# Two PSUM moves in a three-layer transformer kernel: the banks of the dilated attention, and the second GLA pair's cumulated logarithms

## What is computed

```python
h = x
h = h + hgrn2_mixer(rmsnorm(h), ...)              # 8 heads, chunked linear recurrence
h = h + swiglu_ffn(rmsnorm(h), ...)
h = h + dilated_attention_mixer(rmsnorm(h), ...)  # 3 groups (window, dilation) x 4 heads of 128
h = h + swiglu_ffn(rmsnorm(h), ...)
x = rmsnorm(h)
h = rmsnorm_2(x)                                  # second block: NSA attention beside GLA
merged = gate_a * (nsa_attention(...) @ w_up_nsa) + gate_b * (gla_chunked(...) @ w_up_gla)
x = x + merged @ w_out
x = rmsnorm_2(x + ffn(rmsnorm_2(x)))
```

## Time and profile before

| | |
|---|---|
| median of 3 runs | 2213.12 us (2212.46 to 2219.25) |
| the profiled execution's own time | 2218.95 us |
| its span in the profile | 2217.1 us |
| TensorE busy | 2157.2 us, 97% |
| VectorE, ScalarE, GpSimd busy | 1050.2, 852.3, 1173.3 us |
| granted TensorE clock, mean | 0.99 of 2.4 GHz |
| DMA | 193.3 MB, mean 87 GB/s |

### The profile page before, as it was taken

The page is one execution under the profiler, slowest core; times in us unless marked ns, Lnnn a source line. Parts: engine busy times, 40 slices in busy tenths (PEclk is TensorE's granted clock), DMA queues, the critical chain, the costliest instruction groups (busy, mean ns, idle before and its releaser), DMA issues. The chain is left out here.

```text
span 2217.1 us, 28302 instructions
## 1 busy us (share of the span) xinstructions
PE 2157.2 (97%) x10458; PEld 1779.5 (80%) x10458; DVE 1050.2 (47%) x1483; ACT 852.3 (38%) x1209; POOL 1173.3 (53%) x635
## 2 busy tenths in 40 slices
PE   8999999999999999999999999989999999999997
PEld 6788878888888988778888888778767888888886
DVE  7766774422433047754431446464684344422433
ACT  6565644322233234434321233344664334222222
POOL 5868755554554355535554555473214555554552
PEclk9999999999999999999999999999999999999999
DMA  4112213332332222123332332323101223332331
GB/s 166 58 57 66 65 59 95 95 111 88 95 111 80 86 86 76 58 73 103 95 113 84 97 109 81 126 60 96 67 20 62 100 90 91 102 102 89 95 111 69
DMA packets 52822, 193.30 MB, mean 87 GB/s; under 512 B 6768, under 2 KB 7680, under 8 KB 52480
## 3 DMA queue, kind: packets, MB, share of 16 engines
q1 hardware_dynamic: 50688, 184.95, 26.8%
q10 hardware_dynamic: 2048, 7.19, 0.8%
HBM read 187.92 MB, written 4.19 MB: 87 GB/s over the span
## 5 line engine op out<-in xcount | busy, mean ns | idle before, releaser
L1583 POOL TENSOR_TENSOR w_split<-ring,w_split 128x1024 fp32r<-128x1024 f32 (+3 forms) x327 | 842.8, 2578 | 825.9 <-ACT w_split L1102 825.8
L1102 ACT CAST w_split<-ring 128x1024 fp32r<-128x1024 f32 (+3 forms) x327 | 356.3, 1090 | 1009.0 <-PE ps L414 870.7
L412 PE MATMUL ps<-u_split,w_split 128*128 128x512 f32 x1768 | 707.4, 400 | 15.6 <-DVE u_split L1795 10.7
L414 PE MATMUL ps<-u_split,w_split 128*128 128x512 f32 x1768 | 692.5, 392 | 0.0
L413 PE MATMUL ps<-u_split,w_split 128*128 128x512 f32 x1768 | 692.2, 392 | 0.0
L412 PEld LDWEIGHTS ps<-u_split,w_split 128*128 128x128 f32 x1768 | 334.6, 189 | 93.2 <-issue 18.7
L414 PEld LDWEIGHTS ps<-u_split,w_split 128*128 128x128 f32 x1768 | 334.2, 189 | 71.3
L413 PEld LDWEIGHTS ps<-u_split,w_split 128*128 128x128 f32 x1768 | 334.9, 189 | 69.8 <-issue 3.1
L412 PE MATMUL ps<-hid,w_split 128*128 128x512 f32 x648 | 254.0, 392 | 4.3 <-DVE arena L2080 2.8
L414 PE MATMUL ps<-hid,w_split 128*128 128x512 f32 x648 | 252.7, 390 | 0.0
L413 PE MATMUL ps<-hid,w_split 128*128 128x512 f32 x648 | 252.7, 390 | 0.0
(11 more groups left out here) (312 smaller groups left out, 2608.4 us busy)
## 6 DMA issues: line engine op xcount, KB each, us to landing
ring<-in_w_hgrn SPq DMA_DIRECT2D x32, 512.0 KB, 3.5
ring<-in_w_attn_qk SPq DMA_DIRECT2D x24, 512.0 KB, 3.6
ring<-in_w_merge SPq DMA_DIRECT2D x24, 512.0 KB, 3.2
ring<-in_w_gu0a SPq DMA_DIRECT2D x22, 512.0 KB, 3.5
ring<-in_w_gu0b SPq DMA_DIRECT2D x22, 512.0 KB, 3.5
ring<-in_w_gu1a SPq DMA_DIRECT2D x22, 512.0 KB, 3.6
ring<-in_w_gu1b SPq DMA_DIRECT2D x22, 512.0 KB, 3.5
ring<-in_w_gu2a SPq DMA_DIRECT2D x22, 512.0 KB, 3.6
```

Of the source, the lines that this page charges most:

```text
L412: nc.tensor.matmul(ps[:, bank], ws[:, 0, r, w], act[:, 0, c], start=c == 0, stop=False)
L414: m = nc.tensor.matmul(ps[:, bank], ws[:, 1, r, w], act[:, 0, c], start=False, stop=c == n - 1)
L1102: nc.scalar.copy(ws[:, 0, slot, 0:w], ring[:, r, 0:w]).then_inc(s["w_hi"], 1)
L1583: nc.gpsimd.tensor_tensor(ws[:, 1, slot, 0:w], ring[:, r, 0:w], ws[:, 0, slot, 0:w].bitcast(F32), ALU.subtract).then_inc(s["w_lo"], 1)
```

## The change

In the attention, the query/key tiles 0 to 3 use banks 4 to 7 (`qk_bank`), tiles from 4 on bank `N % 4` as before. Tile 0 waits for the first two value groups, tile 4 for the third, tiles from 8 on for the rotation of the tile four before. The value products go to banks 4, 6 and 7 for groups 0, 1 and 2 (`AO_BANK`), each group after its own copied probabilities. In the output projection the wait for the heads' low parts stands in `attn_out` before the three chunks of each head.

In the GLA part, ScalarE copies the second pair's running sums `la[:, 1]` to bank 3 after the gates' eviction. The second pair's level and end exponents read the row from there; the reference columns are still read from SBUF.

```diff
+        AO_BANK = (4, 6, 7)
+
+        def qk_bank(N):
+
+            return 4 + N if N < 4 else N % 4
...
             def qk_tile(N):
-                if N >= 4:
+                if N >= 8:
                     pe.wait_ge(s["rope_sin"], 2 * (N - 3))
-                elif N == 0:
-                    pe.wait_ge(s["av_ready"], GROUPS * TT)
-                used(unit("attn_qk", N, us, N % 4))
+                elif N % 4 == 0:
+                    pe.wait_ge(s["av_ready"], (3 if N else 2) * TT)
+                used(unit("attn_qk", N, us, qk_bank(N)))
...
                 for c in range(6):
                     g, j, w = c % 3, 2 * second + c // 3, slice(c * P, (c + 1) * P)
+                    if c % 3 == 0:
+                        pe.wait_ge(s["ao_lo"], GROUPS * (j + 1))
...
-                    pe.wait_ge(s["pt_ready"], 3 * j + (n + 1 if g == 0 else 3))
+                    pe.wait_ge(s["pt_ready"], 3 * j + n + 1)
                     for b in range(TT):
-                        o = ps[:, 4 + g, b * P:(b + 1) * P]
+                        o = ps[:, AO_BANK[g], b * P:(b + 1) * P]
...
-                    pe.wait_ge(s["ao_lo"], GROUPS * 2)
                     for k in range(4):
                         attn_out(k)
                 attn_core(j)
-            pe.wait_ge(s["ao_lo"], GROUPS * HPG)
...
+
+            act.wait_ge(s["ngate_ready"], TT)
+            act.wait_ge(s["cum"], HEADS_H + 2)
+            nc.scalar.copy(ps[:, 3], la[:, 1]).then_inc(s["cum"], 1)
...
-            def level_exponents(b, dv, l):
+            def level_exponents(b, dv, l, whole=None):
 
                 m = 1 << l
-                bb = b.rearrange("p (b h m) -> p b h m", h=2, m=m)
+                bb = (b if whole is None else whole).rearrange("p (b h m) -> p b h m", h=2, m=m)
                 x = dv[:, l].rearrange("p (b h m) -> p b h m", h=2, m=m)
-                ref = bb[:, :, 0, m - 1:m].broadcast_to((P, T // (2 * m), m))
+                ref = b.rearrange("p (b h m) -> p b h m", h=2, m=m)[:, :, 0, m - 1:m].broadcast_to((P, T // (2 * m), m))
...
                 for l in {1: (6, 5), 2: (4, 3), 3: (2, 1), 4: (0,)}.get(n, ()):
-                    level_exponents(la[:, 1], gdec, l)
+                    if l == LEVELS - 1:
+                        dve.wait_ge(s["cum"], HEADS_H + 3)
+                    level_exponents(la[:, 1], gdec, l, ps[:, 3])
...
             gather_pair(0, next_pair)
             dve.wait_ge(s["kt_ps"], HEADS_H + 1)
-            end_exponents(la[:, 1], gdec)
+            end_exponents(la[:, 1], gdec, ps[:, 3])
```

More of the change, by code:

```diff
@@ L1340, in take_raw @@
                     act.wait_ge(s["qk_ready"], N - 1)
-                nc.scalar.copy(raw[:, N % 2], ps[:, N % 4]).then_inc(s["raw_ready"], 1)
+                nc.scalar.copy(raw[:, N % 2], ps[:, qk_bank(N)]).then_inc(s["raw_ready"], 1)
             def exps(j, g):
@@ L1378, in _ @@
                     act.wait_ge(s["ao_ps"], 3 * j + n + 1)
-                    nc.scalar.copy(in_order(ao_split[:, 0, g * HPG + j]), by_query(g, ps[:, 4 + g])).then_inc(s["ao_hi"], 1)
+                    nc.scalar.copy(in_order(ao_split[:, 0, g * HPG + j]), by_query(g, ps[:, AO_BANK[g]])).then_inc(s["ao_hi"], 1)
             act.wait_ge(s["qk_ready"], 24)
@@ L1913, in cumulate, with end_exponents @@
                 dve.wait_ge(s["cum"], cnt(it, 1, 1))
-            def level_exponents(b, dv, l):
+            def level_exponents(b, dv, l, whole=None):
                 m = 1 << l
-                bb = b.rearrange("p (b h m) -> p b h m", h=2, m=m)
+                bb = (b if whole is None else whole).rearrange("p (b h m) -> p b h m", h=2, m=m)
                 x = dv[:, l].rearrange("p (b h m) -> p b h m", h=2, m=m)
-                ref = bb[:, :, 0, m - 1:m].broadcast_to((P, T // (2 * m), m))
+                ref = b.rearrange("p (b h m) -> p b h m", h=2, m=m)[:, :, 0, m - 1:m].broadcast_to((P, T // (2 * m), m))
                 nc.vector.tensor_tensor(x[:, :, 0], ref, bb[:, :, 0], ALU.subtract)
                 nc.vector.tensor_tensor(x[:, :, 1], bb[:, :, 1], ref, ALU.subtract).then_inc(s["dec_in"], 1)
-            def end_exponents(b, dv):
+            def end_exponents(b, dv, whole=None):
                 b2 = b.rearrange("p (c t) -> p c t", c=NCH)
+                w2 = b2 if whole is None else whole.rearrange("p (c t) -> p c t", c=NCH)
                 nc.vector.tensor_tensor(dv[:, L_END].rearrange("p (c t) -> p c t", c=NCH),
-                                        b2[:, :, C - 1:C].broadcast_to((P, NCH, C)), b2, ALU.subtract
+                                        b2[:, :, C - 1:C].broadcast_to((P, NCH, C)), w2, ALU.subtract
                                         ).then_inc(s["dec_in"], 1)
@@ L2093, in rope @@
                     src, dst = slice(lower, lower + 64), slice(64 - lower, 128 - lower)
-                    nc.vector.tensor_tensor(tsin[dst, N % 2], ps[src, N % 4], sin_a[src], ALU.mult
+                    nc.vector.tensor_tensor(tsin[dst, N % 2], ps[src, qk_bank(N)], sin_a[src], ALU.mult
                                             ).then_inc(s["rope_sin"], 1)
@@ L2153, in ao_rest @@
                     low = ao_low(g, j).rearrange("p b (m r) -> p b m r", r=RESIDUES)
-                    nc.vector.tensor_tensor(low, by_query(g, ps[:, 4 + g]), in_order(ao_split[:, 0, g * HPG + j].bitcast(F32)),
+                    nc.vector.tensor_tensor(low, by_query(g, ps[:, AO_BANK[g]]), in_order(ao_split[:, 0, g * HPG + j].bitcast(F32)),
                                             ALU.subtract).then_inc(s["ao_lo"], 1)
```

## The result

The changed kernel takes **2196.99 us** in the median of 4 runs (2196.22 to 2198.17); the kernel before, beside it, took 2212.79 us (2211.91 to 2219.25). The ratio is 0.9918, with a 95% interval of 0.9898 to 0.9939: 15.8 us off where 17.5 were forecast, and 2197.0 us where 2195.6 were.

The account below looks back on a forecast made before the run. TensorE, busy 97% of the span, was taken as the bound, so gains come only from idle or low-clock time. 5.08 + 2.20 + 1.10 + 1.40 + 8.74 - 1.0 = 17.5 us off 2213.12 gives 2195.6 us; 8-in-10 range 2189.5 to 2204.5.

Parts of the forecast that it names:

- first query/key tile: Attention start: new banks remove tile 0's wait for the value eviction, 3.46 us, and 1.62 of low clock: 5.08 us.
- value products, heads 0 and 1: Attention: each group waits only for its own probabilities' copy, removing 1.10 us in each of two heads: 2.20 us.
- head 2, with the clock behind the longer wait: Attention: early start gains 0, passing into the wait before head 3's scores; the longer wait's low clock costs 1.0 us.
- head 3 and projection: Attention's end: value-product wait gone, 1.10 us; output projection's wait hidden behind head 2's products, 1.40 us.
- GLA exponents: GLA scores: PSUM input keeps exponents short, removing a 4.93 us wait and the low clock behind it: 8.74 us.
- rival (c): First query/key tile: the new banks gain nothing because tile 1 waits for weights instead; 2200.7 us, 5%.
- rival (b): GLA: stretched position additions before the scaled output give back 0 to 8.5 us, middle 4.3; 2199.9 us, 12%.
- The assumption on the base: Whole kernel: gain subtracted from the median 2213.12 us; the profiled execution's extra 5.8 us not shown in these stretches.
- (a): GLA: exponents stay stretched because the reference still comes from SBUF, so 8.74 us is lost; 2204.4 us, 8%.
- (e): Behind head 3's wait: TensorE stays at the low clock through products and projection, kernel slower, up to 2227.6 us; 3%.
- (d): Larger gain: longer wait costs no clock, and low-clock stretches further on shrink by 4.3 us; 2190.3 us, 4%.

Follow-up runs that it names:

- after: The changed kernel with the whole change, against the kernel before: 2196.99 us, ratio 0.9918; its profiled execution took 2196.44 us.
- after again: The changed kernel, unedited, measured and profiled a second time against the kernel before: 2197.86 us, ratio 0.9909.
- before again: The kernel before, unedited, profiled a second time: 2217.75 us, beside a median of 2219.13 us.
- GLA only: The kernel before with only the running sums' copy to PSUM and the exponents reading it: 2206.44 us, ratio 0.9945.
- copy in SBUF: The kernel before with the GLA part alone, but the running sums copied to an SBUF tile instead of PSUM: 2218.57 us, ratio 1.0003.
- one product: The kernel before with one unused small product added at the fourth block norm near 1030 us: 2220.03 us, ratio 1.0007.
- two products: The kernel before with two unused small products added at the fourth block norm near 1030 us: 2220.78 us, ratio 1.0009.
- tile banks only: The kernel before with only the first four query/key tiles' banks and their waits changed: 2210.66 us, ratio 0.9966.
- head 2 waits again: The changed kernel, but head 2's value products wait for all three probability copies again: 2197.24 us, ratio 0.9909 against the kernel before.
- all heads wait again: The changed kernel, but all four heads' value products wait for all three probability copies again: 2202.34 us, ratio 0.9926 against the kernel before.
- attention only: The kernel before with the attention part of the change alone, GLA as before: 2207.29 us, ratio 0.9946.
- fourth rope under the exponentials: The changed kernel with the next head's fourth-tile rope moved ahead of the last exponentials' weighting: 2194.02 us, ratio 0.9891 against the kernel before.
- sixth rope first as well: The kernel with the fourth tile's rope moved, plus the sixth tile's copy and rope moved earlier: 2195.05 us, ratio 0.9895 against the kernel before.

## Why the prediction was right, and where its sizes were off

The terms of the sum against the ledger of after, profile to profile:

| term | predicted | measured |
|---|---|---|
| first query/key tile | 5.08 | 5.3 (the same in the others with it) |
| value products, heads 0 and 1 | 2.20 | 2.7 |
| head 2, with the clock behind the longer wait | 0 - 1.0 | -0.9 |
| head 3 and projection | 1.10 + 1.40 | 3.0 |
| GLA exponents | 8.74 | 8.9 (8.9 alone) |
| sum | 17.5 | 19.0 |
| behind the change | 0 | 2.7 (0.5 in after again) |

**First tile.** Right in mechanism and size. Tile 1's weights were in hand (rival (c) didn't occur), and the version with this edit alone shows 5.3 us. The missing 0.2 us are in how the wait was read: 3.46 us counts from the modelled end of the last value product, 0.40 us behind its start, where the next would have started 0.23 us behind it. By the starts it is 771.29 - 767.44 - 0.23 = 3.62 us, and 5.24 with the 1.62 of low clock.

**Value products.** Right in mechanism; the term was mis-sized. 1.10 us of idle time was read from the trace and taken as the price; the ledger has 1.4 for each of heads 0 and 1, and the version with all four waits back has the same. So a wait of 1.1 us costs 0.3 us more than its bracket says. The timelines show where, here for head 2, before and after:

```profile
934.06 1.91 PE L706 MATMUL ps<-ident_sb,arena 128*128 128x128 f32 x16
...
938.96 0.61 PE L718 MATMUL ps<-arena 128*128 128x128 f32 x4
```
```profile
925.31 1.91 PE L714 MATMUL ps<-ident_sb,arena 128*128 128x128 f32 x16
927.06 1.95 PE L723 MATMUL ps<-arena 128*128 128x128 f32 x16
928.85 0.61 PE L726 MATMUL ps<-arena 128*128 128x128 f32 x4
```

From the first transpose to the first product of the last group it is 938.96 - 934.06 = 4.90 us before and 928.85 - 925.31 = 3.54 after, 1.36 less. From the transposes' start to the products' start (937.07 before) it is 3.01 against 1.75: 1.26 us, of which the bracket shows 1.10, as it counts from the modelled end of the last transpose. The other 0.10 are the 16 records behind the wait, 1.89 us against 1.79. The 0.5 us missing at head 3 and the projection, where two waits went, are of the same size; they were not taken apart.

**Head 2.** Right. The early start went into the next wait whole (4.74 us forecast, 5.01 found, by the same reading of the bracket), and putting it back changed no median. The timelines of TensorE show it, the last key product, the scores and the projection's first product, before and after:

```profile
933.83 0.39 PE L414 MATMUL ps<-u_split,w_split 128*128 128x512 f32 x1
...
950.60 0.60 PE L696 MATMUL ps<-ao_split,w_split 128*128 128x512 f32 x1
```
```profile
925.08 0.39 PE L420 MATMUL ps<-u_split,w_split 128*128 128x512 f32 x1
...
942.71 0.59 PE L704 MATMUL ps<-ao_split,w_split 128*128 128x512 f32 x1
```

From the last key product to the scores it is 944.33 - 933.83 = 10.50 us before and 935.58 - 925.08 = 10.50 after, and 10.50 in the version where head 2 waits again: VectorE's chain sets it. From the scores to the projection it is 950.60 - 944.33 = 6.27 before and 942.71 - 935.58 = 7.13 after; this 0.86 is the whole price.

**The price of the longer wait.** The 1.0 us was a choice between 0 and 2.6, and 0.9 was found, but the runs show that it was not the size of the wait that set it. The clock lost at this point over all versions, and the time from the scores' first product to the projection's first:

| version | waits here, us | clock lost, us | scores to projection, us |
|---|---|---|---|
| before, before again, GLA only | 1.1 + 3.6 | 1.7 | 6.3, 6.4, 6.5 |
| copy in SBUF, one product, two products | 1.1 + 3.6 | 1.7 | 5.8, 6.4, 6.2 |
| tile banks only | 1.1 + 3.6 | 3.4 | 7.1 |
| head 2 waits again | 1.1 + 3.6 | 0 | 5.4 |
| all heads wait again | 1.1 + 3.6 | 3.4 | 7.1 |
| attention only, after, after again | 5.0 | 3.4 | 7.1 |
| fourth rope under the exponentials | 3.6 | 0 | 5.4 |
| sixth rope first as well | 2.0 | 1.7 | 6.5 |

With the same waits the clock lost is 0, 1.7 or 3.4 us. It is also not yet time: 1.7 us of it cost 0.4 to 1.2 us here, 3.4 us cost 1.7, since part of a low stretch falls into the wait and the small products lose less than their share. The agreement of the 1.0 with the 0.9 is luck within that range.

**GLA.** Right: the wait and both low-clock terms went, nothing new stands behind the scaled output (rival (b) didn't occur: VectorE's position additions still take 10.69 us, and no wait for them is in the list), and the copy was hidden. That it is the PSUM operand was argued from two lines of the feed-forward, and the version with the copy in SBUF shows it.

```profile
1470.58 10.69 DVE L2258 TENSOR_TENSOR arena<-arena,mixer_consts 64x248 f32<-64x248 f32 x8
```

**The assumption on the base.** The forecast subtracted the sum from the median 2213.12, with the words that nothing shows the profiled execution's 5.8 us to lie in these stretches. They indeed don't. The base itself was weak: 2213 is not where the kernel before mostly stands: beside the later versions 40 of its 44 runs took 2216.7 us or more, with medians of 2219.1, 2218.2 and 2218.1. The granted clock of the four below is 0.991 or 0.992, of most others 0.989 or 0.990. The profile of the version with the copy in SBUF, taken at 2214.55 us, lacks the low stretch near 1560 us and is 4.3 us ahead there. For the kernel before itself there is no profile of an execution near 2213 us, so there it is argued. Two chips gave these medians near 2218; on which chip the first measurement ran isn't on record, so a difference between chips is not excluded either. Against 2218 us the change brings 20.3 us; the profiles have 19.0 in the predicted terms and 0.5 to 2.7 behind them. Against the 2212.8 us of the first measurement it brings 15.8, 3.2 us less than the terms' 19.0: 1.5 of these are low stretches near 1600 and 1660 us, of which the changed kernel has two and the kernel before one, and 1.7 are not placed. The forecast's terms were 1.5 us too small, and this 3.2 us went the other way, so that the gain came out 1.7 us under the forecast. That the two errors nearly cancel is luck. What decides over the stretch at 1560 us in an execution is not explained: it was missing in versions that do and that don't change the GLA's waits, and there in part or whole in after again and all versions built on the changed kernel later.

**Rivals.** (a), (b), (c) and (e) didn't occur; behind head 3's wait the clock was back within 8 us, and the projection's products start 0.23 us apart from 943.14 us on. (d), further low stretches shrinking, occurred in part: 4.2 us show up near 1560 us in the profile of after, but the same stretch is missing in the version with the tile banks alone, so that the change isn't shown to be its cause, and the gain over the first measurement's median doesn't have it. Its other half, that the longer wait costs no clock, didn't occur.

## What to carry to other kernels

Read for each wait what is late next before it is counted: of four equal waits of 1.1 us three counted, at some 1.4 us each, and the one that stood ahead of another wait was worth nothing. An elementwise VectorE instruction that takes twenty times its median beside a busy GpSimd is worth a copy of one input to a PSUM bank, if a bank is free and ScalarE idle. And where a median and a profile differ by more than the edits' small terms, find out what differs between executions first; here one stretch at the low clock, in code that nobody changed, was nearly as large as the second largest term.

## What the runs showed of the hardware

- A 128x256 subtraction on VectorE with two SBUF inputs took up to 8.88 us; in the kernel before it ran from 1460.79 to 1469.66 us, and GpSimd worked beside it without a pause from 1460.56 to 1469.37; with one input in PSUM, the other and the output in SBUF, 0.41 us at the same place, at most 0.47. An SBUF copy as the input doesn't help: 8.88 us. VectorE's predicated copies beside them, mask in SBUF and scores in PSUM, took 0.45 us in the median and up to 0.81 us in both kernels; why was not tried.
- ScalarE's copy of 128x512 into PSUM takes 0.59 us, the same as out of PSUM; the same copy into SBUF took 0.62 us.
- The clock lost in a low stretch was 1.7, 3.4 or 5.1 us nearly everywhere. Behind the attention's scores it doesn't go with the length of the wait ahead (5.0 us: 3.4; 2.0 us: 1.7; 3.6 us: 0 to 3.4), and one stretch of 5.1 us near 1560 us has no wait just ahead of it, only small products. In time it costs less: 3.4 us of clock behind the scores cost 1.7 us, 5.1 us near 1560 us cost 4.2.
- A wait cost more than the idle time in its bracket: 1.36 us for 1.10, since the bracket counts from a matmul's modelled end and the block behind the wait ran 0.10 us longer.
